# Cache scores of a paged latent attention: from columns of the key product to products on VectorE

## The reference

```python
def mla_keys(latent, w_uk, w_uv, k_norm_nope):
    kn = rms_norm((c @ w_uk).reshape(bsz, s, MLA_HEADS, NOPE_DIM), k_norm_nope)   # 8 heads x 128

def mla_scores(qn, qr, kn, kr):
    s = jnp.einsum('bqhd,bkhd->bhqk', qn, kn) + jnp.einsum('bqhr,bkr->bhqk', qr, kr)
    return s.astype(jnp.float32) * MLA_SCALE

def page_block(phys):                       # for each of the 16 pages of each of the 8 sequences
    kn, kr, v = mla_keys(cache_l[phys], w_uk, w_uv, k_norm_nope)
    return partial_softmax(mla_scores(qn, qr, kn, kr), v)      # maximum, sum, weighted values
```

## Time and profile before

| what | us |
|---|---|
| median of 3 runs (lowest, highest) | 1432.32 (1430.38, 1432.69) |
| the profiled execution's own time | 1431.02 |
| its span, first to last instruction | 1429.2 |
| busy in it: PE, PEld | 1413.9, 1339.3 |
| busy in it: DVE, ACT, POOL | 800.7, 872.3, 220.9 |
| largest lines: L2044, L2045, L2046 (key products) | 505.6, 491.7, 491.2 |

### The profile page before, as it was taken

One profiled execution on the slowest core, in us unless ns is written; L12 is line 12 of the kernel. 1 busy time (PEld: TensorE's weight loads), 2 busy tenths in 40 slices (PEclk: granted clock), 3 DMA queues, 4 the chain that ended last, 5 costly groups with the idle time before them and its releaser, 6 DMA issues.

```text
span 1429.2 us, 30941 instructions
## 1 busy us (share of the span) xinstructions
PE 1413.9 (99%) x11108; PEld 1339.3 (94%) x11108; DVE 800.7 (56%) x1651; ACT 872.3 (61%) x2908; POOL 220.9 (15%) x115
## 2 busy tenths in 40 slices
PE   9999999999999999999999999999999999999998
PEld 7889998999999999999989999889999999999998
DVE  5764444556446564555645555645334667777543
ACT  5544778677666686576965667766774453444332
POOL 3011111211122111112321111131231000000000
PEclk9999999999999999999999999999999999999999
DMA  9541325543345543355333463344734565555551
GB/s 283 172 119 31 65 50 118 143 123 80 72 100 129 124 89 87 75 139 122 87 74 92 109 141 68 72 70 91 177 76 152 175 236 177 177 177 176 177 179 59
DMA packets 263731, 173.77 MB, mean 122 GB/s; under 512 B 165465, under 2 KB 212089, under 8 KB 263577
## 3 DMA queue, kind: packets, MB, share of 16 engines
q1 hardware_dynamic: 263266, 171.53, 46.4%
q10 hardware_dynamic: 318, 0.33, 0.1%
HBM read 132.22 MB, written 6.74 MB: 97 GB/s over the span
## 4 chain that ended last, share of the span: by engine, by line
PE 92%; ACT 4%; DVE 2%; issue 1%; DMA 0%; ACTq 0%; POOL 0%; DVEq 0%
PE ps L2044 17%; PE ps L2045 16%; PE ps L2046 16%; PE ps L2479 6%; PE ps L2480 6%; PE ps L2481 6%; PE ps L2082 2%; PE ps L2135 2%; PE ps L2427 2%; PE ps L2428 2%; PE ps L2136 2%; PE ps L2429 2%; PE ps L2137 2%; PE ps L1918 2%; ACT ksq L868 1%
## 5 line engine op out<-in xcount | busy, mean ns | idle before, releaser
L2044 PE MATMUL ps<-ukh,cTh 128*128 128x384 f32 (+1 forms) x1536 | 505.6, 329 | 3.9 <-ACT ksq L868 2.4
L2045 PE MATMUL ps<-ukl,cTh 128*128 128x384 f32 (+1 forms) x1536 | 491.7, 320 | 0.0
L2046 PE MATMUL ps<-ukh,cTl 128*128 128x384 f32 (+1 forms) x1536 | 491.2, 320 | 0.0
L868 ACT ACTIVATE ksq<-ps 128x128 f32<-128x128 f32 x1024 | 269.3, 274 | 181.8 <-PE ps L2046 179.8
L2044 PEld LDWEIGHTS ps<-ukh,cTh 128*128 128x128 f32 x1536 | 289.9, 189 | 22.7 <-issue 18.2
L2045 PEld LDWEIGHTS ps<-ukl,cTh 128*128 128x128 f32 x1536 | 289.2, 188 | 0.9
L2046 PEld LDWEIGHTS ps<-ukh,cTl 128*128 128x128 f32 x1536 | 288.7, 188 | 0.0
L719 POOL TENSOR_TENSOR rk<-kss,mhalf 128x32 f32<-128x32 f32 x32 | 180.4, 5636 | 456.7 <-DVE kss L1708 456.7
L868 ACT ACTIVATION_READ_ACCUMULATOR ksq<-ps 128x1 f32 x1024 | 209.2, 204 | 0.0
L853 ACT ACTIVATE cTr<-turned 128x1024 uint16<-128x1024 uint16 x126 | 174.1, 1382 | 5.9 <-PE ps L2072 3.7
L1049 ACT ACTIVATE wh<-wraw 128x2048 fp32r<-128x2048 f32 x44 | 84.3, 1916 | 131.4 <-PE ps L2481 126.9
(11 more groups left out here) (518 smaller groups left out, 2536.6 us busy)
## 6 DMA issues: line engine op xcount, KB each, us to landing
clat<-cache_mla SPq DMA_DIRECT2D x128, 256.0 KB, 2.6
wraw<-w_in SPq DMA_DIRECT2D x16, 1024.0 KB, 5.1
wraw<-w_up SPq DMA_DIRECT2D x16, 1024.0 KB, 5.2
wraw<-w_down SPq DMA_DIRECT2D x16, 1024.0 KB, 5.1
braw<-w_in SPq DMA_DIRECT2D x24, 512.0 KB, 4.1
crope<-cache_mla SPq DMA_DIRECT2D x128, 32.0 KB, 2.4
sst<-state_gdn SPq DMA_DIRECT2D x32, 128.0 KB, 3.5
gdn_sample<-sst SPq DMA_DIRECT2D x32, 128.0 KB, 2.0
```

Source lines behind the costliest of these rows:

```text
L868: i = nc.scalar.activation(ksq[:, P * h:P * h + P], ps[:, k % 3, P * h:P * h + P], ACT.Square, accum_out=kss[:, n // 4 % 2, n % 4, h0 + h: ...
L2044: mm(out, cTh[:, n % 2, c], ukh[:, c, cols], start=c == 0, stop=False)
L2045: mm(out, cTh[:, n % 2, c], ukl[:, c, cols], start=False, stop=False)
L2046: i = mm(out, cTl[:, n % 2, c], ukh[:, c, cols], start=False, stop=c == 3)
```

## The change

- The key product of a page goes to two banks of 512 columns (24 products), without score columns: `ukh`, `ukl` lose columns 1024 to 1031, and `query_slot`, `first_scores` and `first_parts` go.
- The scores come from DVE: `scored` multiplies a bank (4 heads x 128) by the sequence's queries, one row of 1024 broadcast to all 128 partitions in two halves (`qb`), and `score_sums` sums each head's 128. The bank is free for PE when `scored` has read it (prod_done), which waits for ACT's squares of that bank.
- The queries are no longer projected through w_uk: `ukf`, `ukT`, qcol, `qeff` go. PE turns `qg` into rows (8 small transposes), DVE copies them, SP writes them to a scratch tensor in HBM and reads them back as broadcasts (`query_half`, two a sequence, three buffers).
- The low halves of a page (`cTl`) are taken by GpSimd (`page_low`), which also makes the roots page by page (`page_roots`: affine step and power of 8 elements) in place of once a group; the maximum over partitions stays once a group (`group_max`), now in between.
- Each square of ACT signals by itself, and writes one of three small buffers.
- The rope keys are turned by DMA like the pages: `split_rope` on DVE, `rope_turn` on SP, and ACT's copy reads 16-bit halves from SBUF; `rope_columns` goes.
- `cTr` holds two pages in place of four; other tiles move.

The diff, cut to its core (removed are also, not shown, the functions and loads named above as gone, and PE's calls of them):

```diff
-        KG = [(slice(0, 384), 0, 3, False), (slice(384, 768), 3, 3, False), (slice(768, 1024), 6, 2, True)]
+        KG = [(slice(0, 512), 0), (slice(512, 1024), 4)]
...
+            def rope_turn(gg):
+                sp.wait_ge(S("rplanes_ready"), gg + 1)
+                wait(sp, "rope_ready", gg)
+                sp.dma_start(rturned[:].bitcast(U16).rearrange("p (x n) -> p x n", n=P), rplanes[:].bitcast(U16), transpose=True).then_inc(S("rope_turned"), 16)
...
+            def query_half(h):
+                s_, j = divmod(h, 2)
+                if h >= 3:
+                    sp.wait_ge(S("prod_done"), 32 * ((h - 3) // 2) + 31 + (h - 3) % 2)
+                sp.dma_start(qb[h % 3][:], scratch[s_:s_ + 1, LAT * j:LAT * j + LAT].to_broadcast([P, LAT])).then_inc(S(f"qb_landed{h % 3}"), 16)
+
             def front_loads(i):
+                if i == 1:
+                    sp.wait_ge(S("a_read"), a_count("qrow1"))
+                    sp.dma_start(scratch, qrow[0:NS].rearrange("s g n -> s (g n)")).then_inc(S("scratch_landed"), 16)
+                    sp.wait_ge(S("scratch_landed"), 16)
+                    query_half(0)
+                    query_half(1)
...
+                if i % 8 == 0:
+                    rope_turn(i // 8)
+                if (i % 32 == 4 and i > 32 or i % 32 == 31) and i // 16 + 2 < 2 * NS:
+                    query_half(i // 16 + 2)
...
-            def group(gg, y):
-                g.wait_ge(S("ms_ready"), gg + 1)
-                nc.gpsimd.tensor_tensor(rk[:, y], kss[:, y], mhalf[:], ALU.pow).then_inc(S("rk_ready"), 1)
+            def page_low(n):
+                g.wait_ge(S("ct_hi"), n + 1)
+                wait(g, "group_done", 2 * (n - 1))
+                nc.gpsimd.tensor_tensor(cTl[:, n % 2], raw_page(n), cTh[:, n % 2].bitcast(F32), ALU.subtract).then_inc(S("ct_lo"), 1)
+
+            def page_roots(n):
+                x = kss[:, n // 4 % 2, n % 4]
+                g.wait_ge(S("squared"), 8 * n + 8)
+                nc.gpsimd.tensor_scalar(x, x, 1.0 / 128, EPS, ALU.mult, ALU.add).then_inc(S("ms_ready"), 1)
+                g.wait_ge(S("ms_ready"), n + 1)
+                if n >= 8:
+                    g.wait_ge(S("s_half"), n // 4 - 1)
+                nc.gpsimd.tensor_tensor(rk[:, n // 4 % 2, n % 4], x, mhalf[:, 0], ALU.pow).then_inc(S("rk_ready"), 1)
+
+            def group_max(gg, y):
                 g.wait_ge(S("s_ready"), gg + 1)
                 nc.gpsimd.tensor_tensor(gate[:], mhalf[0:1, 0, 0:1], mhalf[0:1, 0, 0:1], ALU.add)
                 nc.gpsimd.partition_all_reduce(smax[:].rearrange("p t h -> p (t h)"), ssc[:, y].rearrange("p t h -> p (t h)"), P, RMAX).then_inc(S("smax_ready"), 1)
 
-            for gg in range(NG):
-                group(gg, gg % 2)
+            page_low(0)
+            for n in range(NT):
+                if n + 1 < NT:
+                    page_low(n + 1)
+                if n:
+                    page_roots(n - 1)
+                if n % 4 == 1 and n > 1:
+                    group_max(n // 4 - 1, (n // 4 - 1) % 2)
+            page_roots(NT - 1)
+            group_max(NG - 1, (NG - 1) % 2)
 
...
+                wait(act, "ct_lo", n - 1)
...
             def squares(n, j):
-                k, (_, h0, count, scored) = 3 * n + j, KG[j]
+                k, (_, h0) = 2 * n + j, KG[j]
                 act.wait_ge(S("group_done"), k + 1)
-                if j == 0 and n % 4 == 0:
-                    wait(act, "rk_ready", n // 4 - 1)
-                    wait(act, "s_half", n // 4 - 1)
-                wait(act, "ksq_ready", k)
-                if scored and n >= 4:
-                    nc.scalar.activation(sparts[:, n // 4 % 2, n % 4, :], ps[:, k % 3, P * count:P * count + H], ACT.Copy)
-                for h in range(count):
-                    i = nc.scalar.activation(ksq[:, P * h:P * h + P], ps[:, k % 3, P * h:P * h + P], ACT.Square, accum_out=kss[:, n // 4 % 2, n % 4, h0 + h:h0 + h + 1])
-                i.then_inc(S("ksq_ready"), 1)
+                if j == 0:
+                    wait(act, "rk_ready", n - 7)
+                for h in range(4):
+                    m = 4 * k + h
+                    wait(act, "squared", m - 2)
+                    i = nc.scalar.activation(ksq[m % 3], ps[:, k % 3, P * h:P * h + P], ACT.Square, accum_out=kss[:, n // 4 % 2, n % 4, h0 + h:h0 + h + 1]).then_inc(S("squared"), 1)
 
             def turned_rope(gg):
-                act.wait_ge(S("rope_done"), gg + 1)
+                act.wait_ge(S("rope_turned"), 16 * (gg + 1))
                 wait(act, "rope_scored", gg)
-                nc.scalar.activation(rpT[:], ps[:, B_ROPE, 0:2 * P], ACT.Copy).then_inc(S("rope_ready"), 1)
+                nc.scalar.activation(rpT[:].bitcast(U16).rearrange("p (m t x) -> p x m t", x=2, m=2), rturned[:].bitcast(U16).rearrange("p (x m t) -> p x m t", x=2, m=2), ACT.Copy).then_inc(S("rope_ready"), 1)
...
-            def split_lo(n):
-                v.wait_ge(S("ct_hi"), n + 1)
-                wait(v, "group_done", 3 * (n - 1))
-                V.tensor_tensor(cTl[:, n % 2], cTr[:, :, tokens(n)], cTh[:, n % 2].bitcast(F32), ALU.subtract).then_inc(S("ct_lo"), 1)
...
+            def split_rope(gg):
+                u0 = 4 * gg % RING
+                for u in range(u0, u0 + 4):
+                    v.wait_ge(S(f"page_landed{u}"), 32 * (4 * gg // RING) + 32)
+                wait(v, "rope_turned", 16 * gg)
+                V.tensor_copy(rplanes[:].bitcast(U16).rearrange("p (x l) -> p x l", x=2), crope[:, u0:u0 + 4, :].rearrange("p u l -> p (u l)").bitcast(U16).rearrange("p (l x) -> p x l", x=2)).then_inc(S("rplanes_ready"), 1)
+
+            def scored(n, j):
+                k, h = 2 * n + j, 2 * (n // 16) + j
+                if n % 16 == 0:
+                    v.wait_ge(S(f"qb_landed{h % 3}"), 16 * (h // 3 + 1))
+                v.wait_ge(S("squared"), 4 * k + 4)
+                wait(v, "page_scored", n)
+                V.tensor_tensor(prod[:, j], ps[:, k % 3], qb[h % 3][:], ALU.mult).then_inc(S("prod_done"), 1)
+
+            def score_sums(n):
+                v.wait_ge(S("prod_done"), 2 * n + 2)
+                V.tensor_reduce(sparts[:, n // 4 % 2, n % 4], prod[:].rearrange("p j (h d) -> p (j h) d", d=P), AX, ALU.add).then_inc(S("page_scored"), 1)
...
+                v.wait_ge(S("page_scored"), 4 * gg + 4)
+                v.wait_ge(S("rk_ready"), 4 * gg + 4)
...
-            split_lo(0)
             split_planes(2)
+            split_rope(0)
             for n in range(NT):
                 g, t = n // 4, n % 4
                 beside(2 * n)
-                if n + 1 < NT:
-                    split_lo(n + 1)
-                if n and n % 16 == 0:
-                    query_slot(n // 16)
-                if n == 4:
-                    first_parts()
+                if n == 1:
+                    scored(0, 0)
+                if n:
+                    scored(n - 1, 1)
+                    score_sums(n - 1)
                 if t == 1 and g >= 1:
                     scaled(g - 1)
                 if t == 1 and g >= 2:
@@ -1701,11 +1722,15 @@
                 beside(2 * n + 1)
                 if n + 3 < NT:
                     split_planes(n + 3)
+                if n:
+                    scored(n, 0)
+                if t == 3 and g + 1 < NG:
+                    split_rope(g + 1)
                 if t == 2 and g >= 2 and g % 4 == 1:
                     latent_sum(g // 4 - 1)
-                if t == 3:
-                    v.wait_ge(S("ksq_ready"), 3 * n + 3)
-                    V.tensor_scalar(kss[:, g % 2], kss[:, g % 2], 1.0 / 128, EPS, ALU.mult, ALU.add).then_inc(S("ms_ready"), 1)
+
+            scored(NT - 1, 1)
+            score_sums(NT - 1)
...
-                k, (cols, _, count, scored) = 3 * n + j, KG[j]
-                if scored and n >= 4:
-                    cols = slice(cols.start, cols.stop + H)
-                    pe.wait_ge(S("slot_ready"), n // 16 + 1)
-                out = ps[:, k % 3, 0:cols.stop - cols.start]
+                k, cols = 2 * n + j, KG[j][0]
+                out = ps[:, k % 3]
                 if chunks[0] == 0:
                     pe.wait_ge(S("ct_lo"), n + 1)
-                    wait(pe, "ksq_ready", k - 2)
+                    wait(pe, "prod_done", k - 2)
...
-                pe.wait_ge(S("qeff_ready"), 1)
+                pe.wait_ge(S("qrope_ready"), 1)
+                wait(pe, "s_ready", gg)
...
+                    pe.wait_ge(S("qg_ready"), 1)
+                    for g in range(2):
+                        p_ = begin_a(f"qrow{g}")
+                        for q in range(4):
+                            j = nc.tensor.transpose(p_[0:NS, P * q:P * q + P], qg[:, 4 * g + q, :], ident)
+                        a_done(j)
```

More of the change, by code:

```diff
@@ L1021, in _ @@
                 squares(n, 1)
-                squares(n, 2)
             z_high(2)
@@ L2309, in front_pe @@
                     a_done(j)
-                if i == 2:
-                    pe.wait_ge(S("qg_ready"), 1)
```

(7 more changed lines are left out.)

152 lines of the change are left out of this document (44 added, 108 removed).

## The result

The changed kernel takes 1652.2 us in the median (1651.9 to 1661.4) against 1432.6 (1430.4 to 1432.8) of the kernel before: a ratio of 1.1555, 95% interval 1.1535 to 1.1574. It is slower by 220 us where the forecast had 137, and 24 us above the range's upper end.

The account below looks back on a forecast made before the run. PE, busy 99% of the span, was taken to bound the kernel. 1431.0 - 25 (PE) + 140 (waits for GpSimd) + 20 (clock) + 1.5 (first queries) = 1567.5, with the median's 1.3 above it 1569 us; range 1475 to 1628.

Parts of the forecast that it names:

- the range's upper end: Slow end of the forecast, 1628: way back of 7.5 us and a clock falling three times in four, summed to 1629.
- the first and second rivals: GpSimd's configuration change after the reduce is free (chance 0.15, 1430 us, VectorE's lag +6) or costs half (0.12, 1474 us).
- Page_low after each reduce with issue as the reason: Sign in GpSimd's queue: low halves start some 6 us after the reduce's end, with "issue" as the reason.
- the clock under 9 in slices: Sign on PE: PEclk under 9 in slices of the loop if the waits bring the clock down.
- GpSimd's row past 50%: Sign in the changed profile: GpSimd's row passes 50% once the gaps are added.
- the wait: PE waits for GpSimd's low halves once a group: 19.7 us of queue against 15.15, 31 x 4.5 = +140 us.
- The waits above the mean: Clock term for PE's rests once a group: +20 us, between 0 and 31 x 1.7 = 53.
- PE's savings: Work and waits taken off PE, together -25 us; key products -8, rope transposes -7.4, first scores -3.9.
- the rope part: Two rope transposes a group leave PE, 0.23 us each, over 32 groups: -7.4 us.
- VectorE, "0 to 15": VectorE's scoring rises from 4.3 to 6.3 us a page, hidden by PE's waits; without that cover 0 to 15 us.
- Low halves beside VectorE: Rival: GpSimd's low halves wait behind VectorE, 2.6 us instead of 1.35, in half of the chains twice: +37, 1606 us; chance 0.05.
- the constant power: Rival: GpSimd's power doesn't shrink with its elements, 41.3 us a group against 30.3, 1760 us; chance 0.05.

Follow-up runs that it names:

- e1: Changed kernel without the maximum over partitions (GpSimd copies the scaled scores instead): 1427.4 us, beside 1430.1 of the kernel before.
- e3: Changed kernel with all low halves back on VectorE; roots, maximum, scoring and rope by DMA stay changed: 1448.6 us.
- e5: Kernel before with one part of the change alone, the low halves of every page on GpSimd: 1585.0 us against 1432.4.
- e6: Kernel before with a second reduce, a 1 x 1 memset and a 1 x 1 add on GpSimd behind each reduce but the last: 1430.4 us.
- e8: Kernel before with the rope keys turned by DMA alone, without PE's two transposes a group: 1428.9 us against 1432.4, ratio 0.9978.
- e12: Changed kernel with the maximum taken by PE and VectorE, and the parting of a page's 16-bit halves moved to GpSimd: 1450.6 us, ratio to before 1.0124.
- e10: Changed kernel with the maximum over partitions taken in full by PE and VectorE in place of GpSimd: 1447.8 us, ratio to before 1.0103.
- e7: Changed kernel with PE's 16 high-half products first in pages t = 3, the 8 that need cTl last: 1536.2 us.
- e4: Changed kernel with 20 more products of 512 columns on PE filling the wait before each page t = 3: 1624.7 us.

## Why the prediction was wrong, step by step

- **The mechanism was right,** the forecast's and not a rival's: the queue of GpSimd, both changes of configuration in front of the low halves of t = 3, once a group. e1, e3, e5 and e6 show it from four sides, and the first and second rivals (free or half way back) are out with 7.2 to 7.4 us measured. "Page_low after each reduce with issue as the reason", the waits before pages t = 3 (not page 3 itself, which has no reduce in front, and 0.6 to 13.3 us long where I had 2 to 9), the products' interval (0.228, from 644.83 to 645.97 in five steps, against 0.234) and the clock under 9 in slices came as written. GpSimd's row past 50% "once the gaps are added" too: 454 + 210 + 214 = 878 of 1660.
- **Two terms of the sum failed, by nearly the same amount: the clock by 46 us and the wait by 49. The clock is the worse of the two in proportion,** +20 taken, +65.6 measured, above the bound of 53 as well. I had priced a fall at 1.7 us, half of a 3.4 us stretch from the earlier trace rows. Nearly every wait brought a fall (29 stretches), and most lasted 6.8 or 10.2 us: 232 us in all, of which PE was busy 135 (its half is the 67.3 of the ledger). "The waits above the mean" was a guess about how many, but the larger error was in the length, for which one short event stood.
- **The wait was mis-sized,** 140 against 189. From the end of the high halves to PE's next product I had 17.6 us; the mean of 31 is 19.6: low halves 1.3 (1.35 forecast), roots and semaphores 2.2 (1.7), gate to reduce 7.2 (7.0), way back 7.4 (6.1), low halves 1.3. Two us more, once a group, make 62. Against that the high halves ended 1.7 after the first key product of t = 1, not 2.1, which takes 12 off; the two pages lasted 15.2, as forecast (15.15). So 6.1 a group and not 4.5. The way back taken equal to the way out was the larger half of the two us. The power of 8 elements took 1.71 us, not 1.37, so it has a fixed part of about 0.45 (5.49 = 0.45 + 32 x 0.157).
- **PE's savings:** 24 forecast in the loop, of which 21 were work by the ledger's split (1.2 was a wait, 1.7 clock); 30.0 of work measured. The key products saved more: from start to next start they take 5.74 us a page in e1 and 5.85 in the kernel before (means over 300 to 1000, rests left out), so 14 and not 8; the rope part less, 6.0 and not 7.4 (e8).
- **VectorE, "0 to 15":** 6.7 us in the changed kernel, under the cover of PE's waits; with the cover gone 21 us of rests and 5 of clock (e1). The first rival priced this lag at 6. With neither gap in the queue the kernel ends at 1427 all the same (e1), since PE's saving was larger too.
- **Low halves beside VectorE:** median 1284 ns, mean 1309, maximum 2002. In total 3 us: that rival is out, and so is the constant power. But I had looked at one side only. VectorE's instructions were lengthened, by 22 us in the changed kernel's loop (shown under e12), and the sum has no term for it; how much of it PE felt isn't measured. The Trainium skill has this rule (SBUF — State Buffer, section SBUF: two separate sides): the two engines lock a shared pair of ports for a whole instruction, a VectorE instruction with two SBUF inputs against a GpSimd one that reads SBUF, and the one that starts second waits. The trace agrees on VectorE's side: 25 of the 34 stretched instructions read two SBUF operands (the other 9, copies and products with a scalar, read one), and the 256 products of VectorE, which read one operand from PSUM, never took over 0.69 us.
- **Slips in the sum** that change nothing: the first rival's lightest groups are short by 1.6 (13.6 against 12.0), not 1.9, and the range's upper end leaves out the 2.8 us that the other sums add.
- The profiled execution is 9 us above its median, so the ledger is that much above the verdict.

The range's upper end (1629) had nearly the right wait, 183, but a clock of 40 where 66 came, and nothing for the 7 of other waits: its clock was built from the same short event as the forecast's.

## What to carry to other kernels

An instruction's own duration says little of GpSimd where two kinds of its instructions alternate: here 0.5 us of reduce occupied the queue for 14 us, and what TensorE waited for stood behind it. Before work is moved to such a queue, put a 1 x 1 instruction of that kind behind the old one, where nobody waits (e6): it gives the hidden price for no time. Look also at what the moved work does to the engine that it was taken from: e12 freed VectorE of its copies and stretched 31 more of its instructions than e10. A rest of TensorE costs more than its length (here 0.35 us on top of each us), so reorder to shorten rests first (e7), or fill them (e4).

## What the runs showed that I had not expected

- A memset behind the reduce doesn't pay the change of configuration (0.1 us), an add does (7.2): the gap belongs to the first instruction that carries the change, not to the end of the reduce, and not every other instruction carries it.
- GpSimd copied 128 x 1024 16-bit halves with a stride in 1.06 us (e12), less than it took to subtract 128 x 512 floats (1.3).
- 145 us of useless products made the kernel 27 us faster (e4).
- Taking 6% of VectorE's busy time away by giving the work to GpSimd (568 to 532) didn't shorten TensorE's rests (e12).
- A VectorE instruction of 0.18 us took 1.0 beside GpSimd's subtraction and ended with it; 34 such made 22 us in the changed kernel, and none is in e3.
